# A four-layer encoder trunk: attention's end reordered, weights of the memory attention normalised on GpSimd and turned off TensorE

## The chip, the cores and the metric

The kernel runs on one core of a Trainium2 chip. The metric is the device time of one execution in microseconds. TensorE multiplies matrices into PSUM, VectorE and ScalarE work element by element, GpSimd does small or side work, and SyncE (SP) issues all of the kernel's transfers.

## What is computed

The reference is a trunk of four post-norm layers over 256 tokens of width 1024, in float32. Layers 0 and 3 mix tokens by differential attention (six heads, two softmaxes each), layer 1 by a two-way gated linear recurrence (HGRN2, six heads), layer 2 by a gated short convolution. In every layer a memory attention runs beside the mixer, four heads of 64 into 256 memory tokens. Mixer and memory attention share one input projection and one output projection `w_o`; then come a layer norm, a gated convolutional FFN and a second norm.

```python
p = x @ w_in
mixed = _diff_attention(...) | _hgrn2(...) | _short_conv(...)
recalled = _memory_attention(p[..., tail:], mem, mem_w_kv[layer])
y = concatenate([mixed, recalled], -1) @ w_o[layer]
x = _layer_norm(ALPHA * x + y, ...)
x = _layer_norm(ALPHA * x + _conv_ffn(x, ...), ...)

# memory attention
probs = softmax(einsum('bshd,bmhd->bhsm', q, km))
recalled = einsum('bhsm,bmhd->bshd', probs, vm)
# differential attention, for each head
w = probs[:, 0] - lam * probs[:, 1]
o = einsum('bhqk,bkhe->bqhe', w, v);  o = _rms_norm(o, subln) * (1 - lam_init)
```

## The kernel before

**Weights.** All weight matrices come as one stream of chunks, each of two units (halves) of 128x1024 float32, 512 KB. SP loads a unit into a ring of five raw buffers. ScalarE rounds it to `w_hi` (L1127), VectorE takes the remainder `w_lo = raw - w_hi` (L1365), and TensorE forms three products for each exact one: hi x hi, lo x hi and hi x lo. The split buffers are a ring of five too: the rounding of unit u waits until TensorE has finished unit u-5 (L1126), and the load of unit u waits for the remainder of unit u-5. In a narrow projection half a chunk is 24 matmuls on 128x256, in `w_o` it is 12 on 128x512.

**Order.** `make_schedule` (L68) writes one list of items by hand. Every engine goes through this same list and does its own part of each item, in order, waiting on semaphores; so the list is the order of work on every queue. `chunk` (L83) puts down: the rounding and remainder of a unit four ahead, the first half's matmuls, the items `between`, the rounding and remainder of the next unit, the second half's matmuls with the chunk's eviction, the items `after`. The table `at` says which items stand at which half: slot 2n between the halves of the layer's n-th chunk (behind the query projection of the memory attention, XQ), slot 2n+1 behind it. Layer 0 has two more chunks, so its slots are shifted by four. A chunk that is `held` splits no unit between its halves and does only the first 128 tokens.

**Memory attention.** For two pairs of heads each: `xlog` (logits on TensorE, row maxima on VectorE), `xexp` (exponentials and row sums on ScalarE), `xprob` (VectorE: reciprocal of the row sums, L1627, then one product of 128x1024, L1629). The weights must then be turned, keys onto partitions. In layers 0, 2 and 3 this is `xswap` and `xfetch`: VectorE turns blocks of 32x32 (L1654, into `ex`), SP stores the result to HBM in four transfers (L718) and fetches it back in one, with blocks exchanged (L729; it waits for the stores at L728). In layer 1 it is `xturn`: eight transposes of 128x128 on TensorE for a pair (L1018), evicted by ScalarE in two instructions (L1313). `xpv` multiplies by the memory's values (L1047), and VectorE splits the result (L1370, L1371). The exponentials of a head of the token attention that reuse a buffer `ex` wait until its last user is done (`ex_free`, L604).

**Token attention.** For each of six heads: `log`, `exp`, `prob`; heads 0 to 3 are turned through HBM as above (`swap`, `fetch`), and GpSimd exchanges the last blocks (`spread`, L1736); heads 4 and 5 are turned on TensorE (`turnw`, L1030). `pv` (L1063) multiplies by the values; ScalarE evicts a pair of heads (L1322) and sums its squares (L1325). `ms` scales the sums (VectorE, L1663) and takes the power -1/2 (GpSimd, L1732), `tok` multiplies by it (VectorE, L1669), `scale` turns the pair on TensorE (L1090), from where ScalarE writes `mixT_hi` (L1331) and VectorE `mixT_lo` (L1679).

**Output projection.** Four chunks of `w_o` in the order memory attention, pair 0, pair 1 (held), pair 2. The first half of each waits for its pair's `mixT_lo` (L792). The last takes the held half's work on the other tokens too and ends in the norm.

**Banks.** `turnw`, `scale`, `pv`, `xpv`, `xturn` and the recurrence's levels share two PSUM banks, `SIDE`. TensorE, before it writes one, waits until the previous user's result has been read (`side`, L740). `scale 0` and `turnw` use bank 0, `pv 2` and `pv 3` bank 1.

**Recurrence.** For each of three pairs of heads nine `level` items stand at consecutive slots (7 to 15 for pair 0). A level is eight matmuls (L1109), three products on VectorE that extend keys and queries (L1481 to L1486), a masked copy of the result (L1705), and a ScalarE copy of keys (L1341). Levels alternate between the two banks.

Of the kernel before, what the change touches and what calls it, by code (L numbers as in the profile page):

```python
# [25 lines left out]
P = 128  # L26
SEQ = 256
# [36 lines left out]
def make_schedule():  # L64
# [17 lines left out]

    def chunk(form, role, layer, index, between=(), after=(), held=False):  # L83

        c = len(chunks)
        chunks.append((form, role, layer, index))

        levels = role in ("FF", "FB", "HQ", "HV", "HG")
        split_units(2 * c + AHEAD)
        items.append(("half", c, 0))  # L90
        if levels:
            round_early(2 * c + 1 + AHEAD)
        items.extend(between)
        items.extend(late)
        late.clear()
        if role in LATER:
            late.append((LATER[role], c))
        if not held and c > 1:
            split_units(2 * c + 1 + AHEAD)
        items.append(("half", c, 1))  # L100
        if c == 1:
            split_units(2 * c + 1 + AHEAD)
        if levels:
            round_early(2 * c + 2 + AHEAD)
        items.extend(after)

    for q in range(4):
# [3 lines left out]
    for layer in range(DEPTH):  # L111
# [7 lines left out]
        if kind == "attn":  # L119
# [4 lines left out]
            at = {0: [it("xlog", 0), it("xlog", 1)], 1: [it("xexp", 0)],  # L124
                  2: [it("xexp", 1), it("xprob", 0), it("xswap", 0), it("xfetch", 0)],
                  3: [it("xprob", 1), it("xswap", 1), it("xfetch", 1)],
                  5: [it("log", 0), it("log", 1)], 6: [it("exp", 0)], 7: [it("exp", 1)],
                  8: [it("prob", 0), it("swap", 0)],
# [5 lines left out]
                  15: [it("tok", 0), ("seed", 2 * layer, 1), it("exp", 5), it("prob", 4)],  # L134
                  16: [it("spread", 2)],
                  17: [it("scale", 0), it("prob", 5), it("spread", 3)],
                  18: [it("turnw", 4), it("pv", 2), it("pv", 3), it("turnw", 5)],
                  19: [it("pv", 4), it("pv", 5), it("ms", 1), it("tok", 1), it("ms", 2)], 20: [it("scale", 1), it("tok", 2)],
                  21: [it("scale", 2)]}
            at[14].append(("seed", 2 * layer, 0))  # L140
# [6 lines left out]
        elif kind == "conv":  # L147
            order = [("F", "CG", 0), ("F", "CG", 1), ("F", "CB", 0), ("F", "CG", 2), ("F", "CG", 3), ("F", "CB", 1),
                     ("F", "CG", 4), ("F", "CG", 5), ("F", "CB", 2)]
            at = {0: [it("xlog", 0), it("xexp", 0), it("xlog", 1), it("xexp", 1), it("xprob", 0), it("xswap", 0), it("xfetch", 0)],  # L150
                  6: [it("xprob", 1), it("xswap", 1), it("xfetch", 1)], 13: [it("xpv", 0), it("xpv", 1)]}

            at.update({15: [("seed", 2 * layer, 1)], 16: [("seed", 2 * layer, 0)]})
        else:
            order = []
            for p in range(PAIRS):
                order += [("F", "FF", p), ("F", "FB", p), ("F", "HQ", p)]
            order += [("T", "HV", 0), ("T2", "HV", 1), ("T2", "HV", 2)]
            order += [("F", "HG", p) for p in range(PAIRS)]
            at = {0: [it("xlog", 0), it("xexp", 0), it("xlog", 1), it("xexp", 1)], 1: [it("xprob", 0), it("xprob", 1)],  # L160
                  4: [it("xturn", 0)], 5: [it("xpv", 0)], 6: [it("xturn", 1)], 7: [it("xpv", 1)]}
            at[26], at[28] = [("seed", 2 * layer, 0)], [("seed", 2 * layer, 1)]
# [21 lines left out]
        for n, (form, role, index) in enumerate(order):  # L184
            chunk(form, role, layer, index, between=at.get(2 * n, []), after=at.get(2 * n + 1, []),
                  held=role == "WO" and index[0] == 2)

# [49 lines left out]
def trunk_kernel(nc, stream, x, x_t, mem_t, rel_bias, ln, lam, subln, lower, hnorm, cconv, fconv,  # L237
# [39 lines left out]
    prob_ord = {(items[pos][0][:-4],) + items[pos][1:]: n for n, pos in enumerate(prob_pos)}  # L277

    swap_count, swap_ord, turned_ord, seen = {}, {}, {}, {}
    for item in items:  # L280
# [8 lines left out]
    def weights_of(item):  # L289

        return prob_ord[("x" if item[0][0] == "x" else "",) + item[1:]]
# [53 lines left out]
    with ExitStack() as ctx:  # L345
# [3 lines left out]
        def sem(name):  # L349
            return ctx.enter_context(nc.semaphore(name))  # L350
# [151 lines left out]
        qk_ready, v_ready, value_done = sem("qk_ready"), sem("v_ready"), sem("value_done")  # L502
        logits_done, max_ready, exp_ready = sem("logits_done"), sem("max_ready"), sem("exp_ready")
        xprob_ready, xprob_turned, xprobT_ready, swapped = sem("xprob_ready"), sem("xprob_turned"), sem("xprobT_ready"), sem("swapped")
        prob_ready, prob_turned, probT_ready = sem("prob_ready"), sem("prob_turned"), sem("probT_ready")
# [844 lines left out]
        def _(dve):  # L1350
# [170 lines left out]
            for pos, item in enumerate(items):  # L1521
# [90 lines left out]
                elif name in ("xprob", "prob"):  # L1612
# [3 lines left out]
                    if n >= 2:  # L1616
# [8 lines left out]
                        elif h == 0 and layer_kind(layer) != "attn":  # L1625
                            dve.wait_ge(xpv_done, 2 * layer + 1)
                    link(v.reciprocal(row_inv[:, s, :], row_sum[:, s, :]))  # L1627
                    if name == "xprob":
                        last = v.tensor_tensor(prob[:, s].rearrange("p i t s -> p (i t) s"),  # L1629
                                               ex[:, s].rearrange("p i t s -> p (i t) s"),  # L1630
                                               row_inv[:, s, :].rearrange("p (j one) -> p j one", one=1).broadcast_to([P, 4, SEQ]),
                                               ALU.mult)
                        if n in swap_count:
                            link(last)
                        else:
                            last.then_inc(xprob_ready, 1)
                    else:
                        lj = 0 if item[1] == 0 else 1
                        v.tensor_scalar(row_inv[:, s, 2:4], row_inv[:, s, 2:4], minus_lam[:, lj:lj + 1], None, ALU.mult)
                        for t in range(TT):  # L1640
                            last = v.tensor_scalar(prob[:, s, 1, t, :], ex[:, s, 0, t, :], row_inv[:, s, t:t + 1], None,
                                                   ALU.mult)
                        link(last)
                        for t in range(TT):
                            last = v.scalar_tensor_tensor(prob[:, s, 0, t, :], ex[:, s, 1, t, :], row_inv[:, s, 2 + t:3 + t],
                                                          prob[:, s, 1, t, :], ALU.mult, ALU.add)
                        if n in swap_count:
                            link(last)
                        else:
                            last.then_inc(prob_ready, 1)  # L1650
                elif name in ("xswap", "swap"):
                    n = weights_of(item)
                    of = prob[:, n % 2] if name == "xswap" else prob[:, n % 2, 0:1]
                    v.transpose(swap_source(n).rearrange("p (b c j) -> p c b j", b=4, j=32),  # L1654
# [55 lines left out]
        def _(pool):  # L1710
# [8 lines left out]
            for pos, item in enumerate(items):  # L1719
# [8 lines left out]
                elif name == "ms":  # L1728

                    p, u = item[2], ordinal[pos]  # L1730
                    pool.wait_ge(ms_eps_ready, u + 1)
                    nc.gpsimd.tensor_tensor(ms_r[:, p, :], ms_eps[:, p, :], minus_half[:], ALU.pow).then_inc(ms_r_ready, 1)  # L1732
                elif name == "spread":
                    n = prob_ord["", item[1], item[2]]
# [98 lines left out]
```

## Time and profile before

| | us |
|---|---|
| median of 3 runs | 1243.83 (1242.46 to 1243.92) |
| the profiled execution | 1243.12 |
| its span | 1241.0 |
| TensorE busy (matmuls) | 1228.3, 99% |
| VectorE busy | 1037.2, 84% |
| ScalarE busy | 720.6, 58% |
| GpSimd busy | 26.8, 2% |

The profile is of one execution; times in it count from the span's start. A busy share doesn't tell how close TensorE is to its best pace; the waits, the chain that ended last and the granted clock do. Layer 0's mixer goes from about 20 to 120 us, layer 1's (the recurrence) from 322 to 465, layer 2's from 672 to 745, layer 3's from 952 to 1047.

### The profile page before, as it was taken

Reading aid. Unit: us, or ns where it says so; the run is one execution under the profiler, and the core shown is the slowest. Engines: PE = TensorE matmul, PEld = TensorE weight load, DVE = VectorE, ACT = ScalarE, POOL = GpSimd, SP = SyncE. Lnnn points to the kernel's source line nnn. Section 1 sums busy time; section 2 is a strip of 40 time slices with the busy share of each in tenths; the row PEclk is TensorE's granted clock in tenths of the full one; section 3 lists DMA queues with packets and bytes.
Section 4 is the critical chain, followed back from the end, with each engine's and each line's share of the span. In section 5 each row is a group of like instructions: output and inputs, shape, how many; then the busy total and the mean of one; then the engine's idle time right before and its main releaser. Section 6 shows DMA issues by size and latency. Waiting matters only on the chain.

```text
span 1241.0 us, 19585 instructions
## 1 busy us (share of the span) xinstructions
PE 1228.3 (99%) x7290; PEld 1076.8 (87%) x7290; DVE 1037.2 (84%) x1613; ACT 720.6 (58%) x1170; POOL 26.8 (2%) x37
## 2 busy tenths in 40 slices
PE   9999999999999999999999999999999999999997
PEld 8988888888999998888889888888888988888886
DVE  6896888889779888988888978988888786988887
ACT  6674765555776546655554546655554674755552
POOL 0011000000000100000000000000000011000000
PEclk9999999999999999999999999999999999999999
DMA  9874575555553344656654774666555673666651
GB/s 339 278 235 160 189 249 190 187 187 169 170 184 123 119 148 166 227 191 201 189 187 170 246 255 167 223 200 194 192 187 174 210 238 113 225 205 199 198 190 53
DMA packets 79993, 239.75 MB, mean 193 GB/s; under 512 B 8694, under 2 KB 24694, under 8 KB 78876
## 3 DMA queue, kind: packets, MB, share of 16 engines
q1 hardware_dynamic: 79900, 238.51, 58.2%
q8 instruction: 58, 0.95, 0.3%
q14 instruction: 35, 0.29, 0.1%
HBM read 232.18 MB, written 6.30 MB: 192 GB/s over the span
## 4 chain that ended last, share of the span: by engine, by line
PE 92%; DVE 3%; ACT 2%; DMA 1%; issue 1%; SPq 1%; DVEq 0%; ACTq 0%
PE pair L844 29%; PE acc L938 21%; PE pair L847 14%; PE pair L876 4%; PE pair L877 3%; PE pair L878 3%; PE acc L844 2%; PE pair L1109 2%; PE acc L919 2%; PE acc L918 2%; PE acc L917 2%; DMA raw<-in_stream 1%; PE acc L847 1%; ACT ex L1304 1%; PE pair L1063 1%
## 5 line engine op out<-in xcount | busy, mean ns | idle before, releaser
L1365 DVE TENSOR_TENSOR w_lo<-raw,w_hi 128x1024 fp32r<-128x1024 f32 x400 | 482.5, 1221 | 89.7 <-ACT w_hi L1127 88.3
L1127 ACT ACTIVATE w_hi<-raw 128x1024 fp32r<-128x1024 f32 x400 | 419.9, 1057 | 220.1 <-PE pair L847 71.2
L844 PE MATMUL pair<-xT,w_hi 128*128 128x512 f32 x1520 | 478.0, 396 | 0.2 <-DVE w_lo L1365 0.2
L847 PEld LDWEIGHTS pair<-xT,w_lo 128*128 128x128 f32 x1520 | 285.6, 188 | 67.2
L847 PE MATMUL pair<-xT,w_lo 128*128 128x256 f32 x1520 | 298.9, 278 | 0.0
L844 PEld LDWEIGHTS pair<-xT,w_hi 128*128 128x128 f32 x1520 | 233.7, 189 | 3.5 <-DVE w_lo L1365 0.4
L1174 ACT ACTIVATE hid<-pair 128x512 f32<-128x512 f32 x88 | 52.6, 598 | 125.6 <-PE pair L847 125.6
L1406 DVE TENSOR_TENSOR hid<-pair,hid 128x512 f32<-128x512 f32 x88 | 60.6, 689 | 48.1 <-ACT hid L1174 47.7
L876 PE MATMUL pair<-xT,w_hi 128*128 128x256 f32 x336 | 97.4, 290 | 0.0
L877 PE MATMUL pair<-xT,w_hi 128*128 128x256 f32 x336 | 95.0, 283 | 0.0
L878 PE MATMUL pair<-xT,w_lo 128*128 128x256 f32 x336 | 95.0, 283 | 0.0
L938 PE MATMUL acc<-w_hi,gT_hi 128*128 128x512 f32 x304 | 94.0, 390 | 0.0
L938 PE MATMUL acc<-w_lo,gT_hi 128*128 128x512 f32 x304 | 93.7, 389 | 0.0
L938 PE MATMUL acc<-w_hi,gT_lo 128*128 128x512 f32 x304 | 93.6, 389 | 0.0
L1227 ACT ACTIVATE cv<-hid,fconv_w 128x256 f32<-128x256 f32 x176 | 79.1, 498 | 16.3 <-DVE hid L1406 16.0
L1382 DVE SCALAR_TENSOR_TENSOR cv<-hid,fconv_w,cv 128x255 f32<-128x255 f32 x176 | 77.3, 481 | 3.1
L1378 DVE SCALAR_TENSOR_TENSOR cv<-hid,fconv_w,cv 128x255 f32<-128x255 f32 x176 | 76.8, 478 | 0.0
L938 PEld LDWEIGHTS acc<-w_lo,gT_hi 128*128 128x128 f32 x304 | 57.1, 188 | 12.2
L938 PEld LDWEIGHTS acc<-w_hi,gT_lo 128*128 128x128 f32 x304 | 57.1, 188 | 11.8
L876 PEld LDWEIGHTS pair<-xT,w_hi 128*128 128x128 f32 x336 | 64.3, 191 | 2.4 <-issue 2.0
L877 PEld LDWEIGHTS pair<-xT,w_hi 128*128 128x128 f32 x336 | 64.4, 192 | 0.0
L878 PEld LDWEIGHTS pair<-xT,w_lo 128*128 128x128 f32 x336 | 64.3, 191 | 0.0
(229 smaller groups left out, 1654.3 us busy)
## 6 DMA issues: line engine op xcount, KB each, us to landing
raw<-in_stream SPq DMA_DIRECT2D x400, 512.0 KB, 4.7
gains<-in_ln SPq DMA_DIRECT2D x8, 1024.0 KB, 8.8
swap_scratch<-ex SPq DMA_DIRECT2D x24, 128.0 KB, 2.6
bias<-bias_scratch SPq DMA_DIRECT2D x2, 1152.0 KB, 8.3
raw<-in_stream SPq DMA_DIRECT2D x8, 256.0 KB, 6.0
swap_scratch<-prob SPq DMA_DIRECT2D x32, 64.0 KB, 4.3
a_sq<-swap_scratch SPq DMA_DIRECT2D x8, 256.0 KB, 2.9
xprobT<-swap_scratch SPq DMA_DIRECT2D x3, 512.0 KB, 3.9
```

The lines of the kernel that those rows point to most:

```text
L844: pe.matmul(bank, w_hi[:, slot, kk * P:(kk + 1) * P], xT[:, kk].rearrange("p a s -> p (a s)"), start=(kk == 0), stop=(kk == KT - 1), skip_ ...
L847: last = pe.matmul(bank[:, 0:SEQ], w_lo[:, slot, kk * P:(kk + 1) * P], xT[:, kk, 0, :], start=False, stop=(kk == KT - 1), skip_group_check ...
L876: pe.matmul(bank, w_hi[:, slot, at], a_hi(k, every), start=(k == 0), stop=False)
L877: pe.matmul(bank, w_hi[:, slot, at], a_lo(k, every), start=False, stop=False)
L878: last = pe.matmul(bank, w_lo[:, slot, at], a_hi(k, every), start=False, stop=(k == KT - 1))
L938: last = pe.matmul(ACC[2 * t + h][:], b(i, tok), w[:, slot, h * 512:h * 512 + 512], start=False, stop=False, skip_group_check=True)
L1127: nc.scalar.activation(w_hi[:, u % SPLIT, :], raw[:, u % RAW, :], ACT.Copy).then_inc(hi_ready, 1)
L1227: last = nc.scalar.activation(cv[:, w, i, :], hid[:, w, i, :], ACT.Copy, scale=fconv_w[:, layer, 1, first + i:first + i + 1])
L1365: v.tensor_tensor(w_lo[:, u % SPLIT, :], raw[:, u % RAW, :], w_hi[:, u % SPLIT, :].bitcast(F32), ALU.subtract).then_inc(lo_ready, 1)
L1378: last = v.scalar_tensor_tensor(dst[i][:, 1:SEQ], src[i][:, 0:SEQ - 1], weights(0, i), dst[i][:, 1:SEQ], ALU.mult, ALU.add)
L1382: last = v.scalar_tensor_tensor(dst[i][:, 0:SEQ - 1], src[i][:, 1:SEQ], weights(2, i), dst[i][:, 0:SEQ - 1], ALU.mult, ALU.add)
L1406: v.tensor_tensor(hid[:, w], PAIR[proj_ord[c] % 2][:, :, 0:SEQ], hid[:, w], ALU.add).then_inc(hid_ready, 1)
```

## The change

In `chunk`, a new argument `late_unit` moves the rounding and remainder of the second unit from between the halves to behind the chunk's `after` items. It is used for the last value chunk of an attention layer.

In the attention layers, the swap and fetch of the memory attention's weights move one slot on; at the end, `pv 2` and `pv 3` come before `turnw 4`, `turnw 5` goes behind the first `w_o` chunk, `pv 4`, `pv 5`, `ms 2` and `tok 2` go to slot 20 behind `scale 1`, and `scale 2` from slot 21 to 22. In the convolution layer the swaps move by one or stay, and the second `xprob` a slot earlier. In the recurrence, `xturn` is gone: swap and fetch stand at slots 2 and 3, `xpv` at 9 and 11 instead of 5 and 7. `xprob` is divided: VectorE takes the reciprocal, GpSimd multiplies, one instruction of 128x256 for each head and token tile; VectorE waits for it at the swap.

```diff
-    def chunk(form, role, layer, index, between=(), after=(), held=False):
+    def chunk(form, role, layer, index, between=(), after=(), held=False, late_unit=False):
...
-        if not held and c > 1:
+        if not held and not late_unit and c > 1:
             split_units(2 * c + 1 + AHEAD)
         items.append(("half", c, 1))
...
         items.extend(after)
+        if late_unit:
+            split_units(2 * c + 1 + AHEAD)
...  # attention
-                  2: [it("xexp", 1), it("xprob", 0), it("xswap", 0), it("xfetch", 0)],
-                  3: [it("xprob", 1), it("xswap", 1), it("xfetch", 1)],
-                  5: [it("log", 0), it("log", 1)], 6: [it("exp", 0)], 7: [it("exp", 1)],
+                  2: [it("xexp", 1), it("xprob", 0)], 3: [it("xswap", 0), it("xfetch", 0), it("xprob", 1)],
+                  4: [it("xswap", 1), it("xfetch", 1)], 5: [it("log", 0), it("log", 1)], 6: [it("exp", 0)], 7: [it("exp", 1)],
...
-                  16: [it("spread", 2)],
-                  17: [it("scale", 0), it("prob", 5), it("spread", 3)],
-                  18: [it("turnw", 4), it("pv", 2), it("pv", 3), it("turnw", 5)],
-                  19: [it("pv", 4), it("pv", 5), it("ms", 1), it("tok", 1), it("ms", 2)], 20: [it("scale", 1), it("tok", 2)],
-                  21: [it("scale", 2)]}
+                  16: [it("spread", 2)], 17: [it("scale", 0), it("prob", 5), it("spread", 3)],
+                  18: [it("pv", 2), it("pv", 3), it("turnw", 4), it("ms", 1)], 19: [it("turnw", 5), it("tok", 1)],
+                  20: [it("scale", 1), it("pv", 4), it("pv", 5), it("ms", 2), it("tok", 2)], 22: [it("scale", 2)]}
...  # convolution
-            at = {0: [it("xlog", 0), it("xexp", 0), it("xlog", 1), it("xexp", 1), it("xprob", 0), it("xswap", 0), it("xfetch", 0)],
-                  6: [it("xprob", 1), it("xswap", 1), it("xfetch", 1)], 13: [it("xpv", 0), it("xpv", 1)]}
+            at = {0: [it("xlog", 0), it("xexp", 0), it("xlog", 1), it("xexp", 1), it("xprob", 0)],
+                  1: [it("xswap", 0), it("xfetch", 0)], 5: [it("xprob", 1)], 6: [it("xswap", 1), it("xfetch", 1)], 13: [it("xpv", 0), it("xpv", 1)]}
...  # recurrence
-            at = {0: [it("xlog", 0), it("xexp", 0), it("xlog", 1), it("xexp", 1)], 1: [it("xprob", 0), it("xprob", 1)],
-                  4: [it("xturn", 0)], 5: [it("xpv", 0)], 6: [it("xturn", 1)], 7: [it("xpv", 1)]}
+            at = {0: [it("xlog", 0), it("xexp", 0), it("xlog", 1), it("xexp", 1)],
+                  1: [it("xprob", 0), it("xprob", 1)], 2: [it("xswap", 0), it("xfetch", 0)], 3: [it("xswap", 1), it("xfetch", 1)],
+                  9: [it("xpv", 0)], 11: [it("xpv", 1)]}
...  # VectorE
-                    link(v.reciprocal(row_inv[:, s, :], row_sum[:, s, :]))
+                    inverse = v.reciprocal(row_inv[:, s, :], row_sum[:, s, :])
                     if name == "xprob":
-                        last = v.tensor_tensor(prob[:, s].rearrange("p i t s -> p (i t) s"), ...)
+                        inverse.then_inc(inv_ready, 1)
...
                 elif name in ("xswap", "swap"):
                     n = weights_of(item)
+                    if name == "xswap":
+                        dve.wait_ge(xprob_ready, xprob_ord[n])
...  # GpSimd
+                elif name == "xprob":
+                    pool.wait_ge(inv_ready, xprob_ord[n])
+                    for i in range(2):
+                        for t in range(TT):
+                            last = nc.gpsimd.tensor_scalar(prob[:, s, i, t, :], ex[:, s, i, t, :], row_inv[:, s, 2 * i + t:2 * i + t + 1],
+                                                           None, ALU.mult)
+                    last.then_inc(xprob_ready, 1)
```

## Rows read from the trace of the kernel before

**Rows 1.** The page's first part: busy us (share of the span) xinstructions.
```profile
PE 1228.3 (99%) x7290; PEld 1076.8 (87%) x7290; DVE 1037.2 (84%) x1613; ACT 720.6 (58%) x1170; POOL 26.8 (2%) x37
```
**Rows 2.** Waits of TensorE, whole span: us in total, times, longest.
```profile
PE pair L1030 <- DVE mixT_lo L1679: 3.7, 2, 2.1
```
**Rows 3.** Windows: length, PE, PEld, DVE, ACT, POOL busy, PEclk, DMA share, GB/s.
```profile
91.97:94.19 2.22, 0.16 (x1) 0.03 (x1) 2.18 (x4) 2.11 (x4) 0.34 (x1) 1.00 0.95 310
95.08:98.49 3.41, 3.41 (x19) 3.41 (x17) 1.88 (x3) 0.94 (x3) 0.00 (x0) 0.50 0.94 334
1020.30:1022.10 1.80, 0.17 (x1) 0.01 (x1) 1.57 (x4) 1.77 (x3) 0.00 (x0) 1.00 0.72 162
```
**Rows 4.** The chain that ended last, layer 0: start us, us, what.
```profile
55.70 1.97 ACT ex L1304 x8
...
93.31 0.75 DVE mixT_lo L1679
```
**Rows 5.** Timeline, layer 0: start us, us, engine, line, op.
```profile
90.61 2.77 DVE L1365 TENSOR_TENSOR w_lo<-raw,w_hi 128x1024 fp32r<-128x1024 f32 x2 [0.19 <-ACT w_hi L1127]
90.87 1.44 POOL L1736 COPY probT<-a_sq 128x512 f32<-128x512 f32 x1 [3.92 <-DMA a_sq<-swap_scratch]
91.90 0.58 ACT L1142 ACTIVATE v_tok<-pair 128x512 f32<-128x512 f32 x1
```
**Rows 6.** Timeline, layer 3, from the last value chunk to the last of `w_o`.
```profile
1018.67 2.36 DVE L1365 TENSOR_TENSOR w_lo<-raw,w_hi 128x1024 fp32r<-128x1024 f32 x2 [0.20 <-ACT w_hi L1127]
1019.96 0.59 ACT L1142 ACTIVATE v_tok<-pair 128x512 f32<-128x512 f32 x1
...
1029.27 0.71 PE L938 MATMUL acc<-w_hi,mixT_hi 128*128 128x512 f32 x2
1031.46 1.01 POOL L1732 TENSOR_TENSOR ms_r<-ms_eps,minus_half 128x4 f32<-128x4 f32 x1 [1.39 <-DVE ms_eps L1663]
1034.19 0.68 DVE L1669 TENSOR_TENSOR a_out<-a_out,ms_r 128x512 f32<-128x512 f32 x1
1035.30 0.60 PE L1090 MATMUL pair<-ident,a_out 128*128 128x128 f32 x4
1035.66 0.71 PE L938 MATMUL acc<-w_hi,mixT_hi 128*128 128x512 f32 x2
1036.73 0.75 DVE L1679 SCALAR_TENSOR_TENSOR mixT_lo<-pair,sub_gain,mixT_hi 128x512 fp32r<-128x512 f32 x1 [0.72 <-ACT mixT_hi L1331]
1038.51 0.39 PE L917 MATMUL acc<-w_hi,mixT_hi 128*128 128x512 f32 x1
```
**Rows 7.** Timeline, recurrence: one `xturn` on TensorE and the next projection.
```profile
340.52 1.03 PE L1018 MATMUL pair<-ident,prob 128*128 128x128 f32 x8
341.31 0.36 PE L876 MATMUL pair<-xT,w_hi 128*128 128x256 f32 x1
```
**Rows 8.** Groups by line and form, VectorE: xcount, busy us, mean ns.
```profile
L1629 DVE TENSOR_TENSOR prob<-ex,row_inv 128x1024 f32<-128x1024 f32 x8 | 9.8, 1225 | 0.3
L1654 DVE STREAM_TRANSPOSE ex<-prob 128x1024 f32<-128x1024 f32 x6 | 7.5, 1245 | 0.2
```
**Rows 9.** GpSimd's instructions by tile: ns min/median/max, first and last start.
```profile
L1736 POOL COPY probT<-a_sq x8: 609/680/1441, 74.1 to 1015.9; 128x512 f32<-128x512 f32 x8
L1732 POOL TENSOR_TENSOR ms_r<-ms_eps,minus_half x9: 1007/1017/1918, 85.4 to 1031.5; 128x4 f32<-128x4 f32 x9
```
**Rows 10.** Timeline, recurrence: the masked copy of level 1, level 2's matmuls.
```profile
360.51 0.74 DVE L1705 COPY_PREDICATED dg<-masks,pair 128x512 f32<-128x512 uint8 x1
...
361.24 1.13 PE L1109 MATMUL pair<-qd,ex 128*128 128x128 f32 x8
```
**Rows 11.** Timeline, VectorE, layer 0: the two swaps of the memory attention.
```profile
41.93 1.25 DVE L1654 STREAM_TRANSPOSE ex<-prob 128x1024 f32<-128x1024 f32 x1
...
46.33 1.25 DVE L1654 STREAM_TRANSPOSE ex<-prob 128x1024 f32<-128x1024 f32 x1
```

More of the change, by code:

```diff
@@ L185, in make_schedule @@
             chunk(form, role, layer, index, between=at.get(2 * n, []), after=at.get(2 * n + 1, []),
-                  held=role == "WO" and index[0] == 2)
+                  held=role == "WO" and index[0] == 2, late_unit=(role, index) == ("V", 2))
         def close(form, role, index, following):
@@ L277, in trunk_kernel @@
     prob_ord = {(items[pos][0][:-4],) + items[pos][1:]: n for n, pos in enumerate(prob_pos)}
+    xprob_ord = {n: k + 1 for k, n in enumerate(n for n, pos in enumerate(prob_pos) if items[pos][0] == "xprob")}
     swap_count, swap_ord, turned_ord, seen = {}, {}, {}, {}
@@ L503, in trunk_kernel @@
         logits_done, max_ready, exp_ready = sem("logits_done"), sem("max_ready"), sem("exp_ready")
+        inv_ready = sem("inv_ready")
         xprob_ready, xprob_turned, xprobT_ready, swapped = sem("xprob_ready"), sem("xprob_turned"), sem("xprobT_ready"), sem("swapped")
@@ L1626, in _ @@
                             dve.wait_ge(xpv_done, 2 * layer + 1)
-                    link(v.reciprocal(row_inv[:, s, :], row_sum[:, s, :]))
+                    inverse = v.reciprocal(row_inv[:, s, :], row_sum[:, s, :])
                     if name == "xprob":
[L1629 to L1636, printed above, removed]
+                        inverse.then_inc(inv_ready, 1)
                     else:
+                        link(inverse)
                         lj = 0 if item[1] == 0 else 1
@@ L1732, in _ @@
                     nc.gpsimd.tensor_tensor(ms_r[:, p, :], ms_eps[:, p, :], minus_half[:], ALU.pow).then_inc(ms_r_ready, 1)
+                elif name == "xprob":
+                    n = prob_ord["x", item[1], item[2]]
+                    s = n % 2
+                    pool.wait_ge(inv_ready, xprob_ord[n])
[4 more added lines that the diff above has]
+                    last.then_inc(xprob_ready, 1)
                 elif name == "spread":
```

## The prediction, made before the result was known

> **What bounds the kernel now.** I read the page's busy times first: TensorE's matmuls cover 1228.3 of 1241.0 us, VectorE 84%, ScalarE 58% [rows 1]. TensorE gives no time back while it is fed, so only its own work and its waits can move the end. The list of TensorE's waits is therefore next, and it is short: one wait of weight is left outside the start, the turning of a weight matrix of a head (`turnw`, L1030) behind VectorE's `mixT_lo`, 3.7 us in two pieces, one for each attention layer [rows 2]. The windows give both pieces and something behind the first. In layer 0 TensorE starts almost nothing from 91.97 to 94.19, 2.22 us; from 95.08 on, less than a microsecond after it has resumed, the granted clock is 0.50 (1.2 GHz) for 3.41 us [rows 3]. In layer 3 the pause is 1.80 us (1020.30 to 1022.10), and the clock stays at 1.00 [rows 3]. At half clock 3.41 us hold 1.7 us of full-rate work, so layer 0's pause costs 2.2 + 1.7 us, layer 3's 1.8.
>
> The chain of waits shows what the first pause is made of: from 55.70 on, where ScalarE takes the exponentials of head 1, it runs through ScalarE and VectorE to `mixT_lo` at 93.31 [rows 4]. In layer 0 the end of attention thus hangs on the two element engines from early on.
>
> The profiled execution took 1243.12 us (span 1241.0 and 2.1 around it); the median of three runs is 1243.83, 0.7 above. I sum against the profiled one and add 0.7.
>
> **The end of attention, part by part.** I call the three chunks of w_o before the last WO0, WO1, WO2, each with two halves, and the last one the final.
>
> *The pause before the pairs.* The old order asks first for `turnw 4`, whose PSUM bank `scale 0` still holds until `mixT_lo` is done. The new order asks first for `pv 2` and `pv 3`, on the other bank. They need the value evictions and heads 2 and 3 spread by GpSimd. In layer 0 the spreading is done at 90.87 + 1.44 = 92.31, and `pv 3` is only reached 0.9 us after 91.97 [rows 5]. The evictions end at 91.90 + 0.58 = 92.48 [rows 5], but `late_unit` now puts one rounding of 1.0 us behind them: 91.5, before 91.97. In layer 3 the same sum gives 1019.96 + 0.59 - 1.0 = 1019.6 [rows 6] against 1020.3. So both pauses go, and with the first its slow stretch: the clock fell only behind a pause of 2.2 us, not behind one of 1.8. Removed: 2.2 + 1.7 in layer 0, 1.8 in layer 3. `mixT_lo 0` and `prob 5` also come 1.2 us earlier on VectorE, since one remainder no longer stands ahead; `turnw 5` a half later then finds its weights ready. The delayed unit is WO1's second half, some 10 us away, and the load that SP ties to it is that of a unit five further on: nothing waits.
>
> *What is late next.* Before, `pv 4, 5` stood ahead of WO1's first half; now they stand behind it, and the norm of pair 2 and `scale 2` stand a half later. Let T be the start of WO1's second half. In layer 3 the old rows give, from the first matmul behind `pv 4, 5` (1029.27, [rows 6]): eviction, squares, mean and power are over at 1031.46 + 1.01, so T + 3.2. `tok 2` takes 0.68 [rows 6]: T + 3.9. VectorE's queue now holds, ahead of `mixT_lo 2`, the remainder of the final's second unit, which `tok 2` has kept waiting, and that of the next chunk's first unit (its rounding waits for WO1's end, T + 2.85, and is done by T + 4). Two such remainders take 2.36 (the pair at 1018.67, [rows 6]): T + 6.3, and `mixT_lo` 0.75 more: T + 7.0. TensorE meanwhile has 12 matmuls of WO1's half (12 take 2.85, 1035.66 to 1038.51), 1.42 for the six of half of WO2, 0.36 for `scale 2` (1035.30 to 1035.66), 1.42 again [rows 6]: T + 6.05. The final waits for `mixT_lo 2`: **a new pause of 1.0 us in each attention layer**. Its bounds: 0.4 if VectorE's queue were empty (2.2 us from `scale 2` at 1035.30 to the end of `mixT_lo`, 1036.73 + 0.75, against 1.78 of TensorE's work, [rows 6]), and 2.2 if one more remainder (1.2) stood in the way. I take 1.0. It is shorter than the 1.8 that left the clock alone.
>
> Net: layer 0 3.9 - 1.0 = 2.9; layer 3 1.8 - 1.0 = 0.8.
>
> **The recurrence's memory attention.** Its weights were turned by 16 transposes on TensorE. Eight of them go from 340.52 to 341.31, where the next projection starts [rows 7]: 0.79, both pairs 1.6 us, all on the path, for TensorE has no idle time there. Four evictions on ScalarE (0.6 each) go too and cover nothing. Added are two VectorE transposes of 1.245, in place of two normalisations of 1.225 that go to GpSimd [rows 8]: VectorE stays level. SP gets eight stores and two fetches and waits for a landing before each fetch. The load behind it starts later, but the matmuls of `xpv` now stand at slots 9 and 11, six slots (over 17 us) behind the swap, and a raw weight has five units of lead: no cost; without that lead it would be the landing, 3 to 5 us.
>
> `xpv` at 9 and 11 now stands among the recurrence's levels. There the slack is small: the mask copy that frees the bank ends at 360.51 + 0.74 = 361.25, and TensorE is at that slot at 361.24 [rows 10]. `xpv` adds 1.0 to TensorE and 0.85 to VectorE per slot, so the two stay in step. I charge 0.1, with bounds of -0.2 and +1.5 (one VectorE slot late at both places). Net 1.5.
>
> **GpSimd's normalisation.** The trace has no GpSimd multiply by a column. From below: the copy of 128x512, 0.61 at its shortest and 1.44 at its longest [rows 9], so four instructions of half that size take 1.2 to 2.9 us a pair. From above: the power on four columns, 1.0 to 1.9 us an instruction [rows 9], so 4 to 8. I take 2, the copy being the nearest in shape. What hides it: the swap has moved half a chunk later, and VectorE has a remainder (1.2) and an eviction (0.8) in between. In layer 0 the normalisation may run from 40.7, 1.2 ahead of the old swap at 41.93 [rows 11]; VectorE reaches the first swap near 43.0 and the second near 46.4, where the old one began at 46.33 [rows 11]. So the second store, which layer 0's chain needs for its exponentials at 55.70 [rows 4], leaves as before. Cost 0. If the cover goes, each microsecond over 2 delays that chain by one to two.
>
> At this place the row and the Trainium skill meet (SBUF — State Buffer, "SBUF: two separate sides"): it says that a VectorE instruction with two SBUF inputs and a GpSimd instruction exclude each other for their whole length. The trace agrees: the copy at 90.87 takes 1.44 and not 0.61, and the two remainders beside it take 2.77 and not 2.36 [rows 5, 6]. By that rule the move would not free VectorE at all, and up to two remainders would stand ahead of a normalisation; rival B is what that would do.
>
> **Sum.** 1243.12 - 2.9 - 0.8 - 1.5 = 1237.9 in a profiled execution, 1238.6 as a median.
>
> **Rivals.**
> A. The final doesn't wait: if the norm's chain finished a unit earlier, the 2 x 1.0 would not be paid: 1236.6. Against it: the order in VectorE's queue is fixed by the items. 12%.
> B. GpSimd at 4 us a pair: four multiplies at half the copy's 0.61, and a VectorE remainder of 1.2 ahead of two of them. The store of the second pair leaves 2 to 3 us late, layer 0's chain with it, and `pv 2` waits 2 us at 91.97 for the values: the gain of layer 0 shrinks to 0.9 or, with the slow stretch back, to nothing. 1240.6 to 1241.9, I take 1241.0. For it: layer 0's chain has no slack; against: the copy's rate. 13%.
> C. The recurrence's levels lose a VectorE slot at both `xpv`: 1.4 more, 1240.0. 7%.
> D. Slower. GpSimd at the power's rate, 7 us a pair: VectorE stands at the swap, in all four layers, and everything queued behind it, remainders above all. In layer 0 `exp 1` comes some 7 us late and the pause before `pv 2` is 6, with the slow stretch; in layer 3 some 4. That is 12 paid against 7.3 removed (3.9, 1.8 and 1.6), and the 2.0 of the final still due: near 1250. It decides from about 1.1 us per GpSimd instruction. 8%, as a multiply isn't a power.
>
> **How the numbers follow.** The forecast has 60%, its own range 1237.5 to 1239.7. The 8 in 10 reach from A to B: 1236.3 to 1241.8. A measurement of this kernel tells 0.2%, 2.5 us, from no change; the line is 1241.3. Faster: 58 of the forecast, 12 of A, 6 of B, 5 of C: 0.81. Slower: D's 0.08. Same: what is left, 0.11.
>
> **What would show it.** No wait at L1030, and `pv 2` starting right behind WO0's first half; the clock at 1.00 around 92 to 98; a new wait of about 1 us of the first L917 matmul for `mixT_lo`, twice; no L1018; VectorE's swaps in layer 0 ending near 44.2 and 47.6, no later; four GpSimd multiplies of 0.3 to 0.6 each. The prediction is wrong if those are above 1 us, if the final does not wait, or if matmuls around 357 to 372 have gaps.

## The result, and the profile after

The changed kernel takes 1252.65 us (median of 4 executions, 1250.40 to 1253.84) against 1243.22 for the kernel before: a ratio of 1.0068, 95% interval 1.0055 to 1.0081. It is 9.4 us slower, where the prediction's 1238.6 is 4.6 below the kernel before. The profiled execution took 1250.4 us, with a span of 1248.6. One execution of kernel 8 below ran at a mean granted clock of 0.56 and took 2031.18 us; it is left out of that kernel's numbers.

The page's first part, which answers to [rows 1], has less work on TensorE and 36 us more on GpSimd:

```profile
PE 1226.7 (98%) x7274; PEld 1073.3 (86%) x7274; DVE 1030.4 (83%) x1607; ACT 718.7 (58%) x1166; POOL 62.4 (5%) x69
```

The list of TensorE's waits (us in total, times, longest), where [rows 2] had one wait of weight, is long now. The L1030 wait is gone, and these stand there:

```profile
PE acc L846 <- DVE hid L1414: 2.9, 1, 2.9
PE pair L878 <- DVE qk L1400: 2.4, 2, 1.6
PE pair L1092 <- DVE a_out L1667: 1.8, 1, 1.8
PE pair L1092 <- issue: 1.8, 1, 1.8
PE acc L919 <- DVE mixT_lo L1677: 1.6, 2, 0.8
...
PE pair L1108 <- DVE qd L1454: 1.1, 1, 1.1
PE pair L1111 <- ACT ex L1343: 1.0, 2, 0.6
```

Only L919, the final's wait for `mixT_lo 2`, was in my sum. The windows (columns as in [rows 3]) put the longest of the others at their places: TensorE's bank for the next projection of queries and keys (53.03), `scale 0` in both attention layers (91.18 and 1023.28), and the convolution layer (706.46). The third line is the stretch where the clock was 0.50 before; it is 1.00 here.

```profile
53.03:54.82 1.79, 0.28 (x3) 0.07 (x1) 1.79 (x4) 0.00 (x0) 0.00 (x0) 1.00 1.07 379
91.18:93.10 1.92, 0.39 (x2) 0.00 (x0) 1.90 (x2) 1.92 (x7) 0.37 (x1) 1.00 0.13 36
95.08:98.49 3.41, 3.41 (x26) 3.14 (x25) 3.08 (x8) 3.41 (x6) 0.02 (x1) 1.00 0.95 352
...
706.46:709.60 3.14, 0.28 (x3) 0.08 (x1) 3.07 (x5) 0.43 (x1) 0.00 (x0) 1.00 1.00 410
1023.28:1025.40 2.12, 0.39 (x2) 0.00 (x0) 2.05 (x3) 2.12 (x8) 0.78 (x2) 1.00 0.99 290
```

The new GpSimd instruction, by tile (ns min/median/max, first and last start), against the copy that I had sized it by in [rows 9]:

```profile
L1737 POOL TENSOR_SCALAR prob<-ex,row_inv x32: 921/928/1982, 41.7 to 982.9; 128x256 f32<-128x256 f32 x32
...
  DVE ex L1652: 14.5, 6
```

VectorE stood 14.5 us for it at six of the eight swaps. The timeline of layer 0 shows two of these, with GpSimd's four instructions as one line, and answers to [rows 11]. I had expected the swaps to start near 43.0 and 46.4:

```profile
41.65 4.15 POOL L1737 TENSOR_SCALAR prob<-ex,row_inv 128x256 f32<-128x256 f32 x4 [41.22 <-DVE row_inv L1629]
47.23 4.52 POOL L1737 TENSOR_SCALAR prob<-ex,row_inv 128x256 f32<-128x256 f32 x4 [1.43 <-DVE row_inv L1629]
...
45.83 1.25 DVE L1652 STREAM_TRANSPOSE ex<-prob 128x1024 f32<-128x1024 f32 x1 [1.97 <-POOL prob L1737]
...
51.78 1.25 DVE L1652 STREAM_TRANSPOSE ex<-prob 128x1024 f32<-128x1024 f32 x1 [3.53 <-POOL prob L1737]
```

### The profile page after: what moved, and what is told of

It is laid out like the page before. It is cut to its first block, busy times and chain, and to the rows that moved or that the text cites. A ratio compares the mean times of both kernels' runs of the same rounds, so it can differ in the third digit from the quotient of the medians.

```text
span 1248.6 us, 19583 instructions
## 1 busy us (share of the span) xinstructions
PE 1226.7 (98%) x7274; PEld 1073.3 (86%) x7274; DVE 1030.4 (83%) x1607; ACT 718.7 (58%) x1166; POOL 62.4 (5%) x69
## 4 chain that ended last, share of the span: by engine, by line
PE 80%; DVE 7%; ACT 5%; issue 3%; POOL 2%; DMA 2%; SPq 1%; DVEq 0%; ACTq 0%; POOLq 0%
PE pair L846 27%; PE acc L940 19%; PE pair L849 13%; DVE w_lo L1367 2%; ACT ex L1306 2%; PE acc L919 2%; PE pair L878 2%; PE pair L879 2%; POOL prob L1737 2%; PE pair L880 2%; PE acc L921 2%; PE acc L920 2%; DMA raw<-in_stream 2%; PE pair L1111 1%; ACT w_hi L1129 1%
```

## The experiments

Below, "a pause" is the time between the starts of two matmuls on TensorE beyond what the same pair of lines usually takes. All kernels were timed beside the kernel before, whose median was 1243.1 to 1243.3 in each set. Line numbers shift by one to five between kernels.

**1. The changed kernel without GpSimd's part.**

```diff
-                        inverse.then_inc(inv_ready, 1)
+                        link(inverse)
+                        v.tensor_tensor(prob[:, s]..., ex[:, s]..., row_inv..., ALU.mult).then_inc(xprob_ready, 1)
```

> The changed kernel with one thing undone: VectorE again multiplies by the reciprocal (one product of 128x1024 at xprob), GpSimd does not. Theory G (GpSimd's multiply, 1.12 us an instruction and 4.5 a pair, is the whole of the loss; VectorE stands 14.5 us in all at the swaps): no wait at a swap, no pause near 53, 91, 706 and 986 us and none of over 0.3 us among the recurrence's levels, and the forecast of the rest holds: 1238.6 us, 4.6 under the kernel before. Rival O (the new order of attention's end, or the recurrence's turning, costs something of its own): 1241 or more, and the pause of 1.9 us ahead of scale 0 (L1092) stays. Both expect the pause of 1.0 us before the final chunk of w_o, twice.

Measured: 1247.06 (5 executions, 1245.67 to 1248.67), ratio 1.0032 (1.0019 to 1.0044). GpSimd's part is worth 5.6 of the 9.4 us. The pauses at 53 and in the convolution layer fell from 1.8 and 3.1 to nothing and 0.5. But the pauses at `scale 0` stayed (1.93 and 2.26), and one of 1.8 at the convolution layer's first `w_o` matmul appeared. So GpSimd is the largest cause and not the only one.

**2. The kernel before with GpSimd's normalisation and the moved swaps of layers 0, 2 and 3 alone**, with the old end and the old recurrence.

> The kernel before with only the normalisation on GpSimd and the swaps of layers 0, 2 and 3 where the change has them; the old end of attention, and the recurrence still turns on TensorE. Theory G: the loss without its gains, so the changed kernel's 1252.7 plus the 5.2 that end and turning were forecast to give: 1256 to 1258, with pauses at scale 0 and again at turnw 4 in both attention layers. Rival O: the loss is shared with the end, so 1250 or less.

Measured: 1252.75 (1250.71 to 1253.97), ratio 1.0073 (1.0060 to 1.0086): as slow as the whole change, less than I expected. The `turnw` pause didn't add to the new ones: it vanished. I read it so, that TensorE now stood at `scale 0` just ahead of it and VectorE caught up meanwhile; here the pauses in one chain of work didn't sum.

**3. The kernel before with the new end alone** (`late_unit` and the rows of `at` from slot 16 on).

> The kernel before with only the new order of attention's end and the late unit. Theory G, by the forecast's own terms: 2.2 + 1.7 + 1.8 removed, 1.0 added twice, 1239.5 us; no wait at L1030, the clock at full rate near 92 to 98 us, a wait of 1.0 at the first matmul of the final chunk in layers 0 and 3. Rival O: the pair's norm, moved back, costs more than the pause that went, 1243 or more.

Measured: 1239.80 (9 executions, 1239.39 to 1241.13), ratio 0.9974 (0.9964 to 0.9984). As expected: both `turnw` pauses gone, `scale 0` with 0.2, and the final's wait is there twice, 0.98 each:

```profile
PE acc L917 <- DVE mixT_lo L1679: 1.6, 2, 0.8
```

**4. The kernel before with the recurrence's pairs turned by VectorE and HBM alone.**

> The kernel before with only the recurrence's weights turned by VectorE and HBM and xpv at slots 9 and 11, normalised on VectorE. Theory G: 1.6 us of transposes gone and 0.1 paid among the levels, 1241.8 us. Rival O: xpv among the levels makes level 0 and 1 late on VectorE, as the changed kernel's gaps of 1.3, 0.75 and 0.5 us there suggest, 1243.5 to 1245.

Measured: 1243.09 (11 executions, 1240.58 to 1245.34), ratio 1.0001 (0.9992 to 1.0011). The transposes are gone, and nothing is gained. TensorE's waits show where it went:

```profile
PE pair L1107 <- DVE qd L1453: 1.1, 1, 1.1
...
PE pair L1110 <- ACT ex L1342: 0.5, 2, 0.4
```

With the transposes and both `xpv` gone from ahead of it, TensorE is at level 0 before VectorE has scaled the queries: a pause of 1.29, and 0.8 in two more at the levels behind, which kernel 12 comes back to. I had looked at the levels beside the new slots of `xpv`, not at the one ahead of which TensorE now had less to do.

**What makes `scale 0` late.** That pause is in kernels 1 and 2 and not in 3 and 4. What 1 and 2 share is the memory attention's swaps a slot later. I compared kernels 1 and 3 backwards from `scale 0`, VectorE's instructions one by one. VectorE is 1.8 to 2.3 us later in kernel 1 all the way back to a remainder at 59.26 (kernel 3) and 61.10 (kernel 1); just before that, it is 0.5 *earlier*. The remainder waits for ScalarE, and ScalarE's timeline of kernel 1 names the cause:

```profile
58.05 0.51 ACT L1306 ACTIVATE ex<-lg,neg_max 128x256 f32<-128x256 f32 x1 [2.24 <-DMA swap_scratch<-ex]
```

The exponentials of self-attention's second head go into the buffer `ex` from which the second pair's store reads. In kernel 3 they start at 56.21 without a wait. SyncE's queue shows why the store is late, first in kernel 1, then in kernel 3:

```profile
45.21 2.08 SPq L720 DMA_DIRECT2D swap_scratch<-ex  x4
49.64 0.38 SPq L731 DMA_DIRECT2D probT<-swap_scratch  x1
50.07 1.24 SPq L651 DMA_DIRECT2D raw<-in_stream  x1
51.35 2.17 SPq L720 DMA_DIRECT2D swap_scratch<-ex  x4
```
```profile
43.81 1.78 SPq L718 DMA_DIRECT2D swap_scratch<-ex  x4
47.77 0.38 SPq L729 DMA_DIRECT2D probT<-swap_scratch  x1
48.20 0.51 SPq L649 DMA_DIRECT2D raw<-in_stream  x1
48.74 1.98 SPq L718 DMA_DIRECT2D swap_scratch<-ex  x4
```

The first pair's fetch (second line) leaves 4.0 to 4.4 us after the first of its own stores, for whose landing it waits, and the weight load and the second pair's stores stand behind it. The swap on VectorE began only 0.6 us later in kernel 1 (47.55 against 46.93); its stores left 2.6 us later, since the first pair's stores (the first line) had left 1.4 us later and all that stands behind them took 1.2 longer. Two kernels tested this.

**5. Kernel 1 with the attention layers' swaps back in their old slots.**

```diff
-                  2: [xexp 1, xprob 0], 3: [xswap 0, xfetch 0, xprob 1], 4: [xswap 1, xfetch 1],
+                  2: [xexp 1, xprob 0, xswap 0, xfetch 0], 3: [xprob 1, xswap 1, xfetch 1],
```

> The changed kernel with the normalisation on VectorE (as in e1_vector_norm, 1247.06) and, in the two attention layers alone, the memory attention's swaps, stores and fetches back in steps 2 and 3. Theory B (a buffer): a step later the second pair's store is issued at 51.35 instead of 48.74, because SyncE's queue holds the first pair's fetch ahead of it; it reads the buffer that the exponentials of self-attention's second head fill, ScalarE stands 2.24 us for it at 55.8, VectorE runs 2.1 us late from there to the end of the layer, and scale 0 pauses TensorE by 1.9. With the slots back: no wait on ScalarE there, scale 0 with under 0.5, twice; 1247.1 - 2 x 1.9 = 1243.3. Rival E (the reordered end makes the pause at scale 0): both pauses stand, 1247.

**6. Kernel 1, slots as they are, with the second pair's swapped weights in a buffer of their own.**

```diff
             s = n % 2
+            if <xprob 1 of an attention layer>:
+                return ke[:, s].rearrange("p h s -> p (h s)")[:, 512:1536]
             return (ex[:, s] if items[prob_pos[n]][0] == "xprob" else prob[:, s, 1:2])...
```

> e1_vector_norm (1247.06) with its slots as they are, but the swapped weights of the second pair stand in a buffer of their own in the attention layers, so that the exponentials of self-attention's second head no longer wait for the store. Theory B: ScalarE's wait of 2.24 us is gone though the store is as late as before, scale 0 under 0.5 us, 1243.3 as in g1_slots_back. Rival Q (the moved swaps hold up SyncE's queue, and the weights land later): the buffer changes nothing, VectorE is still 2 us late at 61 us, 1247 here and 1243.3 in g1_slots_back. Rival E: 1247 in both.

Measured: 1243.44 (11 executions, 1242.43 to 1245.81) and 1243.73 (12, 1242.43 to 1247.74), against the 1243.3 expected of theory B. In kernel 6 the store still leaves late (49.94), but from `ke`, and ScalarE starts at once:

```profile
49.94 2.96 SPq L722 DMA_DIRECT2D swap_scratch<-ke  x4
```
```profile
55.58 0.50 ACT L1308 ACTIVATE ex<-lg,neg_max 128x256 f32<-128x256 f32 x1
```

Both pauses at `scale 0` are gone in both kernels. Rival Q fell with kernel 6, rival E with both: one buffer's reuse made the pauses, and taking it away gave 3.6 us in kernel 5 and 3.3 in kernel 6. In the changed kernel itself ScalarE's exponentials in layer 0 wait for VectorE instead (`neg_max`, 8.3 us at the longest), which stood at the swaps; I take the buffer to be the limit behind that one, since it shows once GpSimd's part is taken out.

**7. Kernel 3 with the next stage's first weight unit moved behind `scale 2`.**

```diff
-        split_units(2 * c + AHEAD)
+        if not late_first:
+            split_units(2 * c + AHEAD)
         items.append(("half", c, 0))
...
         items.extend(between)
+        if late_first:
+            split_units(2 * c + AHEAD)
```

> e3_end_alone (1239.8) with the rounding and the remainder of the next stage's first weight unit behind the last mixing transpose on their engines. Theory C (ScalarE and VectorE reach the last eviction late, behind that unit): the pause ahead of the last output chunk falls from 0.98 to about 0.3, twice, 1238.4. Rival T (the transpose and its two evictions are themselves the chain): both pauses stay at 0.9 to 1.0, 1239.8; should the stage behind then lack its first unit, it is 1241.

Measured: 1239.16 (6 executions, 1238.76 to 1240.70), ratio 0.9971 (0.9960 to 0.9982). The pause fell from 0.98 to 0.50, twice, and not to 0.3:

```profile
PE acc L921 <- DVE mixT_lo L1683: 0.7, 2, 0.3
```

Theory C holds in kind. This is the fastest of all kernels tried; against kernel 3 it is 0.6 us, less than a comparison of two medians can vouch for, while the two waits in the trace are plain.

**8. The changed kernel with GpSimd copying in place of multiplying** (the division by the row sums is left out).

> The changed kernel (1252.65) with GpSimd copying the memory attention's weights instead of multiplying them: the division by the row sums is left out. Theory G (the length of GpSimd's instructions is the price): a copy of 128x512 took 0.61, so one of 128x256 takes 0.3 to 0.5 against the multiply's 0.92, a pair under 2 us instead of 4.2; the pauses at 53.03 (1.79) and in the convolution layer (3.1) go, near 1247. Rival H (the hand-over VectorE to GpSimd to VectorE is the price, whatever the instruction's length): VectorE's waits at the swaps stay over 1 us each and the time over 1250. If the copy of 256 columns costs as much as the multiply, nothing changes, 1252.6.

Measured: 1245.25 (median of nine executions, 1242.54 to 1251.51), ratio 1.0022 (1.0009 to 1.0035). GpSimd's instructions and VectorE's wait for them:

```profile
L1737 POOL COPY prob<-ex x32: 394/400/1405, 40.5 to 974.8; 128x256 f32<-128x256 f32 x32
...
  DVE ex L1652: 4.3, 4
```

At the mean of 515 ns an instruction, a pair took 2 us, which is the very figure that I had assumed. VectorE's wait falls from 14.5 to 4.3, the pause at 53 is gone and that of 3.1 is 0.7. The pauses at `scale 0` are there still, 1.0 and 1.7 us. Theory G holds: the multiply's length is the price. It is 1.8 us below kernel 1, so with the slots as the change has them and 2 us a pair, the work on GpSimd costs nothing that these executions show.

**9. The changed kernel with two multiplies of 128x512 for a pair** (the second half of the rows takes the first half's factor).

> The changed kernel (1252.65) with two multiplies of 128x512 for a pair on GpSimd instead of four of 128x256 (the second half of the rows takes the first half's factor). If a multiply is paid by its columns (0.92 for 256: 3.6 ns each), one of these takes 1.8 and nothing changes, 1252.6. If about half of the 0.92 is paid per instruction, one takes 1.4, a pair 2.8 instead of 4.2, and the time lies near 1249.

Measured: 1248.34 (4 executions, 1247.43 to 1249.48), ratio 1.0048 (1.0032 to 1.0063).

```profile
L1736 POOL TENSOR_SCALAR prob<-ex,row_inv x16: 1559/1572/2469, 41.1 to 979.1; 128x512 f32<-128x512 f32 x16
...
  DVE ex L1652: 10.6, 5
```

From 256 columns in 921 ns and 512 in 1559 follow 2.5 ns a column and 0.28 us an instruction: between the two cases that I had named. For the copy, 394 and 609 [rows 9] give 0.84 ns a column and 0.18. The multiply takes three times as long a column as the copy.

**10. Kernel 7 with the convolution layer's swaps moved as in the change.**

```diff
-            at = {0: [xlog 0, xexp 0, xlog 1, xexp 1, xprob 0, xswap 0, xfetch 0], 6: [xprob 1, xswap 1, xfetch 1],
+            at = {0: [xlog 0, xexp 0, xlog 1, xexp 1, xprob 0], 1: [xswap 0, xfetch 0], 5: [xprob 1], 6: [xswap 1, xfetch 1],
```

> g3_end_first_unit (1239.2) with the convolution layer's swaps, stores and fetches moved as the change moves them, the weights normalised on VectorE. Theory S (SyncE's queue): a fetch waits in the queue until its store has landed, and the loads of raw weights wait behind it; a step later ScalarE lacks them (it stood 5.4 and 5.1 us for raw weights at 695 and 716 in g1_slots_back, once 5.5 in g3_end_first_unit), and TensorE pauses at the reuse of the accumulators and at the seeds: 0.57, 1.26 and 1.78 there against 0.37 here. So 1239.2 + 0.6 + 1.3 + 1.4, near 1242.4, no more than 1.3 above that. Rival R (those pauses come down from the recurrence, whose levels run late): 1239.2.

Measured: 1242.37 (11 executions, 1241.14 to 1243.20): 3.2 us lost, the amount that theory S had, and rival R fell. The waits of ScalarE and TensorE between 676 and 730, in this kernel and then in kernel 7:

```profile
ACT w_hi L1131 <- DMA raw<-in_stream: 13.8, 5, 5.3
...
PE acc L942 <- ACT acc L1292: 1.6, 1, 1.6
PE acc L848 <- DVE hid L1416: 0.5, 1, 0.5
PE pair L880 <- DVE hid L1416: 0.5, 1, 0.5
```
```profile
ACT w_hi L1131 <- DMA raw<-in_stream: 7.7, 4, 5.5
...
PE acc L942 <- ACT acc L1292: 0.2, 1, 0.2
```

And SyncE's queue, again this kernel and then kernel 7: the four or five weight loads behind the first fetch leave at 691.05 instead of 686.43.

```profile
687.01 1.78 SPq L722 DMA_DIRECT2D swap_scratch<-ex  x4
690.63 0.38 SPq L733 DMA_DIRECT2D prob<-swap_scratch  x1
691.05 2.69 SPq L653 DMA_DIRECT2D raw<-in_stream  x4
```
```profile
682.40 1.77 SPq L722 DMA_DIRECT2D swap_scratch<-ex  x4
686.01 0.38 SPq L733 DMA_DIRECT2D prob<-swap_scratch  x1
686.43 5.89 SPq L653 DMA_DIRECT2D raw<-in_stream  x5
```

The queue is not the whole of it. VectorE, which turns later here, works without a break from 682.71 to 714.18 and runs 1.4 us behind kernel 7 (`hid`, L1416, at 701.40 instead of 699.98); the pause of 0.5 at 701.97 ends with it. The two later pauses, 0.5 at 721.50 and 1.6 at 729.11, come by the raw weight that ScalarE rounds at 717.97 instead of 714.80. Its load stands behind the second pair's fetch, which leaves at 706.34 instead of 703.04; 1.4 of these 3.3 us are VectorE's later swap, the rest is the stores, which took longer. No kernel parts VectorE's order from the queue. The last of these pauses is 1.6 in all five traces with the moved swap and without GpSimd's multiply (kernels 1, 5, 6, 8 and 10), and between nothing and 1.0 in the six with the old one.

**11 and 12. Kernel 7 with the recurrence's pairs turned as in the change, and the same with `xpv 0` at step 7, ahead of level 0.**

```diff
-                  9: [it("xpv", 0)], 11: [it("xpv", 1)]}
+                  7: [it("xpv", 0)], 11: [it("xpv", 1)]}
```

> g3_end_first_unit (1239.2) with the recurrence's pair turned by VectorE and HBM as in the change. Theory L: 1.6 of transposes go, and the pauses at the levels come back, 1.3 at level 0 (TensorE is there before VectorE's scaled queries) and 0.8 at the next ones: 2.1 - 1.6, 1239.7. Rival F (what e4_turn_alone lost was its own slot's chance): 1237.6.

> As h2_end_and_turn, with the first product of the memory attention at step 7, ahead of level 0, instead of step 9: its 0.8 us of matmuls run while VectorE scales the queries. Theory L: the pause at level 0 falls from 1.3 to about 0.5, 1238.9; by rival F both are 1237.6. If VectorE does that product's two evictions ahead of the queries, the pause stays 1.3 and the time 1239.7.

Measured: 1239.97 (8 executions, 1238.63 to 1241.08) and 1240.37 (11, 1239.36 to 1241.99). Kernel 11 is as theory L had it. Kernel 12 is not: the pause at level 0 has gone, and a longer one stands two levels on, here in kernel 11 and then in kernel 12.

```profile
348.28 0.91 PE L1111 MATMUL pair<-q,ksum 128*128 128x128 f32 x6 [1.14 <-DVE qd L1457]
...
358.30 1.20 PE L1114 MATMUL pair<-qd,ex 128*128 128x128 f32 x8 [0.75 <-ACT ex L1346]
```
```profile
357.32 1.20 PE L1114 MATMUL pair<-qd,ex 128*128 128x128 f32 x8 [1.37 <-ACT ex L1346]
```

The copy that TensorE waits for there is late by SyncE's queue, as in kernels 1 and 10. Its keys were ready at 353.82, but on ScalarE it stands behind a rounding, and that waited for a raw weight; in kernel 12:

```profile
355.54 1.06 ACT L1132 ACTIVATE w_hi<-raw 128x1024 fp32r<-128x1024 f32 x1 [6.11 <-DMA raw<-in_stream]
356.50 0.68 ACT L1346 ACTIVATE ex<-ke 128x512 f32<-128x512 f32 x1
```

The weight's load left at 350.71, right behind the second pair's fetch at 350.29, and that had waited for stores issued from 342.00 on. Kernel 4 has the same: ScalarE stands 5.95 us for a raw weight until 356.52, with the keys ready at 354.95. In kernel 7, which turns on TensorE, ScalarE waits there for the keys. So what kernel 12 saved at level 0 was spent in waiting for the same late weight. This is read from the traces; no kernel moved that load alone, and kernel 11's trace puts the end of ScalarE's wait (356.49, 5.2 us behind the issue of the load) down to TensorE.

## Why the prediction was wrong

The single parts, each measured by one kernel against another, add up to the result: GpSimd's part +5.6 (the changed kernel against kernel 1), the attention layers' swap slot +3.6 (1 against 5), the convolution layer's +3.2 (10 against 7), the turning in the recurrence +0.8 (11 against 7), the new end -3.5 (3 against its own set's 1243.27). The sum is +9.7, and +9.4 was measured; each part is good to about 1 us, and holds for one order of taking the parts out. In another the end is worth little: between kernel 2 and the changed kernel the new end and the turning together give 0.1. I read it so, that the end's 3.5 us are there only when TensorE does not already stand at `scale 0`.

- **The pause before the pairs: right for the end alone.** Both pauses and the slow stretch went; kernel 3 measured 1239.8, where the steps on the end alone give 1243.83 - 3.7 = 1240.1.
- **What is late next: right.** "A new pause of 1.0 us in each attention layer": 0.98, four times (changed kernel and kernel 3). That the rounding and the remainder of the next chunk's first unit make half of it is kernel 7, which moved both.
- **GpSimd's normalisation: the term that was mis-sized.** This is one of the two steps that failed: "I take 2, the copy being the nearest in shape", cost 0. A pair took 4.15 to 4.52 us, in the recurrence 8.8 for two, and the price was 5.6. The bounds of 1.2 to 8 held it; the choice inside did not. Between two far ends I took the one nearest in *shape*, where what differed was the operation. The cover was judged well enough: by kernel 8, 2 us a pair cost nothing. "Decides from about 1.1 us per GpSimd instruction" can't be checked: the mean was 1.12, and by addition alone, without the 6.8 us of the moved slots, the change would stand at 1245.9, 2.7 above before, but no kernel ran so. Rival B had the length of a pair, 4 us, and 13%, for another reason (the copy's rate behind a remainder) and at less than half of the price: 2.4 over the forecast, with only layer 0's chain in it. (Its upper end of 1241.9 doesn't follow from its terms; all 2.9 of layer 0 lost is 1241.5.) Rival D, "near 1250", was closest by its number, with VectorE standing at the swap in all layers, but at 7 us a pair; that its number came nearest, with nothing in it for the moved slots, is luck.
- **"So the second store ... leaves as before": wrong, and the larger error of reasoning.** The moved swaps had no term of their own in the sum. They cost 3.6 in the attention layers and 3.2 in the convolution layer with no GpSimd in them. This is the other step that failed. I had placed VectorE's arrival at the swaps (43.0 and 46.4; it was there at 43.9 and 48.3), but not followed the store behind the fetch that waits for a landing on SyncE's queue, nor the buffer `ex` that the store reads and the next exponentials fill. `ex_free` stood in the text ahead of the prediction.
- **"A raw weight has five units of lead: no cost": wrong.** It was said of the recurrence, and there ScalarE stood 5.95 us for one in kernel 4 and 6.4 in the changed kernel, against 0.7 before; in the convolution layer, where I had not asked, it waited 13.8 us instead of 7.7 (kernel 10). A ring of five holds five only when the queue that fills it isn't held up by something else.
- **The pause at 53, in no step.** VectorE at a swap also holds the eviction of a projection, which frees one of two PSUM banks. The cover of that is one projection, not a ring.
- **The recurrence: the transposes went, but the added 0.1 was wrong.** It was 2.1 in kernel 4: 1.3 at level 0, which I had not looked at, and 0.8 behind the late raw weight.

Not settled: where all of GpSimd's 5.6 us lie. The pauses of the changed kernel's trace give 1.8 at 53, 0.9 at 986 and, in the convolution layer, 3.1 against kernel 1's 0.5 and 1.8: 3.5 in sum. The two profiled executions are only 2.5 apart (1250.40 and 1247.87); the changed kernel's was the fastest of its four. The slower ones, with mean granted clocks down to 0.995 where kernel 1 had 0.998 and 0.999, have no trace. Nor is it known whether GpSimd's normalisation would pay with the old slots, which wasn't tried.

## What to carry to other kernels

Size an operation that the trace lacks by its operation and its columns, and where the rows can't tell a copy from arithmetic, let the price at the slow end decide the forecast's chances. Moving a step later moves every entry it makes in a queue that issues transfers in order; follow each to the buffer that it reads as well as to the one that it fills, and to the loads behind it. Work taken off the busiest engine pays only if the next thing that engine reaches is ready that much sooner.

## What the runs showed of the hardware

**A GpSimd multiply by a per-partition column** of 128x256 float32 took 0.92 us alone. Beside a VectorE remainder it took 1.44 to 1.98: the four of the second pair in layer 0 took 1.81, 0.92, 0.93 and 0.93, the first of them beside the remainder at 47.06 of 1.19. This is the exclusion of the two engines that the Trainium skill names (SBUF — State Buffer, "SBUF: two separate sides"). The trace agrees where VectorE's remainder began first: GpSimd lost 0.5 to 1.1 us, and it was the smaller part of the pair's 4.2 to 4.5. Where GpSimd began first it shows no such lock: the remainders at 41.87, 340.58 and 975.00, each 0.2 to 0.4 us into a multiply, took 1.33, 1.24 and 1.23, against 1.22 as a rule. So the move did free VectorE, which the prediction, by that rule, had ruled out.

**The half-clock stretch of TensorE isn't decided by a pause's length alone.** The prediction had read from two pauses that 2.2 us brings it and 1.8 does not. In kernel 4 a pause of 2.22 us was followed by no such stretch, nor was one of 2.26 in kernel 1; in kernel 2 both pauses of 2.1 to 2.2 were. The windows, as in [rows 3], of kernel 4 and then of kernel 2:

```profile
91.81:94.03 2.22, 0.39 (x2) 0.00 (x0) 2.22 (x3) 1.89 (x4) 0.57 (x1) 1.00 0.91 253
94.90:98.31 3.41, 3.41 (x26) 3.19 (x26) 2.10 (x4) 2.19 (x11) 0.00 (x0) 1.00 0.96 345
```
```profile
90.68:92.97 2.29, 0.39 (x2) 0.00 (x0) 2.29 (x3) 2.29 (x9) 1.27 (x2) 1.00 0.98 325
93.50:96.91 3.41, 3.41 (x10) 2.70 (x9) 3.37 (x6) 3.41 (x6) 0.00 (x0) 0.50 0.60 207
```

The changed kernel's four executions had mean granted clocks of 0.995 to 0.998, the lower clocks with the longer times, which suggests that part of its spread of 3.4 us is how many of these stretches an execution met. A pause near 2 us should be priced with a chance of the stretch, 1.7 us by the 3.41 us at 0.50, and not with a threshold.
